# The low parts of the weights of four groups, made by GpSimd in place of VectorE

## What is computed

```python
h = rms_norm(x, g_mix)
z = h @ w_in + b_in                      # 1024 x 7168
va, ga, xb, gb, sa, sb = split(z)        # xb, gb: 1536 channels each
u = causal_conv31(va * sigmoid(ga))      # 1024 channels
v = rg_lru(causal_conv4(xb), ...)        # gates by block-diagonal products, then a scan over time
y_b = (v * gelu(gb)) @ w_b_out           # 1536 -> 1024
m = sigmoid(sa) * y_a + sigmoid(sb) * y_b
...                                      # output product, feed-forward, second block, final norm
```

## Time and profile before

| what | value |
|---|---|
| median of 3 runs | 2438.41 us (2437.18 to 2440.22) |
| profiled execution | 2438.8 us, its span 2436.6 us |
| TensorE matmul busy | 2410.2 us, 99% of the span |
| VectorE busy | 1405.1 us, 58% |
| ScalarE busy | 822.2 us, 34% |
| GpSimd busy | 2.2 us |
| TensorE clock granted | 0.998 of full over the span |

### The profile page before, as it was taken

How to read it: one execution, slowest core, us unless ns; L and a number is a source line. 1 busy time by engine, 2 the same in 40 slices (tenths; PEclk the granted TensorE clock), 3 DMA queues, 4 the chain that set the end, 5 groups by cost and what they waited for, 6 DMA issues and landing times.

```text
span 2436.6 us, 26080 instructions
## 1 busy us (share of the span) xinstructions
PE 2410.2 (99%) x10904; PEld 1958.8 (80%) x10904; DVE 1405.1 (58%) x1952; ACT 822.2 (34%) x1236; POOL 2.2 (0%) x7
## 2 busy tenths in 40 slices
PE   8999999999999999999999999999999999999998
PEld 6778688687778888888888888888878877888888
DVE  8799599698689734443233232234557544462377
ACT  5552442533513713332032131132333132122355
POOL 0000000000000000000000000000000000000000
PEclk9999999999999999999999999999999999999999
DMA  4202112012131112311111111112211111211232
GB/s 136 57 22 59 55 35 75 26 44 74 35 104 44 44 52 74 91 52 51 45 52 44 52 44 52 50 46 70 78 37 55 44 36 44 56 52 49 73 81 80
DMA packets 225117, 138.38 MB, mean 57 GB/s; under 512 B 13024, under 2 KB 216160, under 8 KB 225000
## 3 DMA queue, kind: packets, MB, share of 16 engines
q1 hardware_dynamic: 225000, 136.72, 19.0%
HBM read 127.75 MB, written 8.95 MB: 56 GB/s over the span
## 4 chain that ended last, share of the span: by engine, by line
PE 88%; DVE 6%; ACT 4%; issue 1%; DMA 0%; SPq 0%; DVEq 0%; ACTq 0%
PE bank L601 27%; PE bank L603 27%; PE bank L602 27%; PE bank L671 2%; DVE q_all L2528 1%; PE bank L912 1%; DVE uw L2318 0%; PE bank L894 0%; ACT whi L1045 0%; ACT bank L1148 0%; DVE wlo L1672 0%; DVE uc L2045 0%; ACT lru L1151 0%; PE bank L941 0%; ACT un_hi L1054 0%
## 5 line engine op out<-in xcount | busy, mean ns | idle before, releaser
L601 PE MATMUL bank<-h_hi,whi 128*128 128x512 f32 x1984 | 782.2, 394 | 10.0 <-DVE wlo L1672 10.0
L603 PE MATMUL bank<-h_hi,wlo 128*128 128x512 f32 x1984 | 774.6, 390 | 0.0
L602 PE MATMUL bank<-h_lo,whi 128*128 128x512 f32 x1984 | 774.4, 390 | 0.0
L601 PEld LDWEIGHTS bank<-h_hi,whi 128*128 128x128 f32 x1984 | 373.7, 188 | 91.5 <-issue 11.9
L602 PEld LDWEIGHTS bank<-h_lo,whi 128*128 128x128 f32 x1984 | 373.7, 188 | 79.4 <-issue 2.9
L603 PEld LDWEIGHTS bank<-h_hi,wlo 128*128 128x128 f32 x1984 | 373.5, 188 | 77.8
L1045 ACT ACTIVATE whi<-raw 128x1024 fp32r<-128x1024 f32 (+1 forms) x211 | 215.2, 1023 | 453.8 <-PE bank L603 419.4
L1672 DVE TENSOR_TENSOR wlo<-raw,whi 128x1024 fp32r<-128x1024 f32 (+1 forms) x211 | 249.5, 1185 | 170.9 <-ACT whi L1045 169.7
L601 PE MATMUL bank<-ff_hi,whi 128*128 128x512 f32 x512 | 199.9, 390 | 0.0
L602 PE MATMUL bank<-ff_lo,whi 128*128 128x512 f32 x512 | 199.5, 390 | 0.0
L603 PE MATMUL bank<-ff_hi,wlo 128*128 128x512 f32 x512 | 199.5, 390 | 0.0
(11 more groups left out here) (365 smaller groups left out, 3105.0 us busy)
## 6 DMA issues: line engine op xcount, KB each, us to landing
raw<-in_w_in SPq DMA_DIRECT2D x92, 512.0 KB, 3.7
raw<-in_w SPq DMA_DIRECT2D x64, 512.0 KB, 4.0
raw<-in_w_b_out SPq DMA_DIRECT2D x16, 384.0 KB, 3.0
raw<-in_w_out SPq DMA_DIRECT2D x11, 512.0 KB, 3.5
x_in<-in_x_t SPq DMA_DIRECT2D x8, 512.0 KB, 7.0
raw<-in_w_a_out SPq DMA_DIRECT2D x8, 512.0 KB, 3.9
raw<-in_w_o SPq DMA_DIRECT2D x8, 512.0 KB, 4.2
xcols<-in_x_t SPq DMA_DIRECT2D x16, 256.0 KB, 2.8
```

Of the source, the lines that this page charges most:

```text
L601: pe.matmul(target, lh, rh, start=start, stop=False, skip_group_check=True)
L602: pe.matmul(target, lh, rl, start=False, stop=False, skip_group_check=True)
L603: last = pe.matmul(target, ll, rh, start=False, stop=stop and point is not None, skip_group_check=True)
```

## The change

The low parts of blocks `("gb", 0, 2)` to `("yb", 3, 3)`, numbers 5 to 57 of the list (37 blocks of 1024 columns and 16 of 768), are made by GpSimd. VectorE's `ahead` passes over them, and makes those of all other blocks as before. GpSimd works through the 53 blocks in their order, each as soon as its high part is made and its buffer is free, between its first clears and its last one.

```diff
+        BY_POOL = range(number["gb", 0, 2], number["yb", NG - 1, 3] + 1)
...
                 while split[0] <= min(k, last_block):
                     i = split[0]
                     split[0] += 1
+                    if i in BY_POOL:
+                        continue
                     raw_, hi, lo = weight_tiles(i)
                     w.wait_ge(*at("w_hi", i))
...
             w = Once(pool)
             for n in range(2):
                 pool.memset(gate_w[n][:], 0.0).then_inc(*up("pool_done", ("gate_w_clear", n)))
+            for i in BY_POOL:
+                raw_, hi, lo = weight_tiles(i)
+                w.wait_ge(*at("w_hi", i))
+                w.wait_ge(*at("used", i - 3))
+                pool.tensor_tensor(lo, raw_, hi.bitcast(F32), ALU.subtract).then_inc(*up("pool_done", ("w", i)))
             w.wait_ge(*at("w1", FC - 1, DT - 1, 1))
             pool.memset(gates_raw[:], 0.0).then_inc(*up("pool_done", ("cleared",)))
```

## The result

The changed kernel took 2465.86 us (median of 4 runs, 2463.29 to 2467.39), the kernel before 2437.8 us in the same comparison: ratio 1.011, interval 1.0098 to 1.0122, so slower by 28 us. The profiled execution took 2466.36 us, 27.6 us more than that of before.

The account below looks back on a forecast made before the run. TensorE, busy 99% of the span, was taken as the bound. To the profiled 2438.8 us came three groups' losses of 4.6 us less 1.9 us (+11.9) and 2.5 us of clock: 2453 us, range 2436 to 2478.

Parts of the forecast that it names:

- the likeliest case: VectorE stands still during each GpSimd subtraction, delaying TensorE at the `yb` banks: 2453 us, chance 0.58.
- The bound and the tight place: TensorE bounds; VectorE delays over about 2 us between 136 and 208 us reach it at `yb` in groups 0 to 2.
- The mutual hold: VectorE and GpSimd share SBUF access; VectorE was taken to stand for each whole GpSimd subtraction, the upper bound.
- Rival 1: No mutual hold: GpSimd works beside VectorE, only the wait for L1913 goes; 2437 us, chance 0.25.
- The time of a subtraction: On GpSimd, 2.06 us for 1024 columns and 1.56 for 768, between VectorE's time and three streams in turn.
- The sum ahead of bank 0: From 136 to 208 us, seven holds of 12.4 us against 6.0 freed: VectorE 6.4 us late, TensorE loses 4.6.
- 6.0 freed: Time off VectorE's queue from 136 to 208 us: six low parts removed, three of 1.13 and three of 0.87 us.
- 1.86 of slack: Group 0, `yb` bank 0: VectorE's read ends at 208.83 us, TensorE takes the bank again at 210.69.
- The clock: TensorE's pauses may halve its clock: 5 us for three groups, of which half, 2.5 us, was taken.
- Group 3: VectorE's waits ahead of the `yb` blocks go, pieces start earlier, and TensorE's 1.9 us wait for L1913 goes.
- The range: 2436 to 2478 us: the hold between its bounds (2437 to 2476) plus no mutual hold, without GpSimd starving.
- Rival 2: GpSimd gets its turn only when VectorE stops; low parts late, some 21 us a group, 2500 us, chance 0.11.

Follow-up runs that it names:

- run 3: Changed kernel, but VectorE again makes the 24 low parts ahead of the tight `yb` banks in groups 0 to 2, GpSimd the other 29: 2435.31 us, ratio 0.9988.
- run 4: Changed kernel, but GpSimd makes only the 24 low parts ahead of the tight `yb` banks in groups 0 to 2, VectorE all others: 2468.56 us, ratio 1.0126.
- run 1: Changed kernel, but GpSimd clears each of the 53 low parts instead of subtracting, so it reads nothing: 2435.29 us, ratio 0.9989.
- run 2: Changed kernel, but GpSimd copies raw into each low part, reading one input instead of two: 2434.65 us, ratio 0.9988.
- run 5: Changed kernel, with 18 convolution pieces in each of groups 0 to 2 moved from ahead of the `yb` blocks to the next group: 2434.83 us, ratio 0.9987.
- run 6: Changed kernel, but GpSimd makes only three low parts in each of groups 0 to 2: 2442.18 us, ratio 1.0018.
- run 8: Kernel before, nothing on GpSimd; in group 3 VectorE's `ahead` at the two sb blocks goes behind the convolution pieces: 2435.49 us, ratio 0.9988.

## Why the prediction was right, and where it was short

2453 us was forecast, with 2436 to 2478 as the range; 2465.86 came. The direction and the likeliest case were right, the size was half: + 14.4 us on the profiled execution, against 27.6.

- *The bound and the tight place.* Right. TensorE waits at `yb` bank 8, for bank 0's read, in groups 0, 1 and 2 alone. Runs 3 and 4 show that the place decides: 29 subtractions elsewhere cost nothing, 24 here cost all.
- *The mutual hold.* Right, and shown: it is there with two inputs (2.14 us) and with one (0.79), and absent when GpSimd only writes (runs 1 and 2), always for VectorE's operations with two inputs. Rival 1 is out for reading operations. The Trainium skill (SBUF — State Buffer, section SBUF: two separate sides) excludes VectorE's two-input instructions only against GpSimd operations that read SBUF; these traces agree, with 0.759 us for the longest `evens` piece of the run with clears and 2.89 us for a piece beside a subtraction.
- *The time of a subtraction.* Nearly right, in part by luck: 2.06 and 1.56 us were taken, the middle of two bounds, for the operation and the hold alike. The operation by itself takes more, 2.34 us (656.66) and 1.84 (705.57), and VectorE stands for less than that: 2.14 (2.08 on the scan) and, at 768 columns, 1.58 at a piece (2.33 in place of 0.75).
- *The sum ahead of bank 0.* This step failed in its count. "From 136 to 208 us seven high parts are made" held for the old timing of bank 0. The holds push that read to 217.50 us, and by then an eighth subtraction, of 1024 columns, has started at 212.16. The prediction added it only on the way to bank 8. Holds measured in group 0 ahead of bank 0: 2.14 + 2.08 + 2.14 + 1.58 + 1.66 + 1.34 + 1.58 + 2.08 = 14.6 us, less 6.0 freed = 8.6; the other 0.75 us of the 9.35 late are small gaps, such as VectorE's wait for its own last piece ahead of L1795, which a low part used to fill. Less 1.86 of slack: 7.5 us (the profile has a wait of 7.30), against 4.6 forecast. Three groups: 22.1 us of waits in place of 13.8. Run 5, where the read comes early and seven subtractions precede it, bears the count out.
- *The clock.* This term was too small. Half of 5 us was taken, and more than the 5 came: 2.4 to 2.5 us a group, 7.5 in all, of which about 0.1 us a group is the first matmul's longer step, which is there at full clock too (run 6). Run 6 has pauses of 1.3 us at a clock of 1.00, so the cost came with the long pauses and not with the short ones; where between them it begins, no run shows. It is not the length of a pause alone: around 1768 us the clock fell with no pause over 0.5 us, behind sixteen matmuls of one column.
- *Group 3.* Right in size and cause: 1.9 us back, and run 8 shows that it is the queue's order.
- *Together:* 22.1 of waits and 7.5 behind them; that is all but 0.1 to 0.2 us a group of the 10.0 us by which each of groups 0 to 2 is longer. The first matmul behind the `yb` blocks comes 10.05, 20.06 and 30.07 us later than before (in groups 1 and 2 at 415.12 and 592.67 us, against 395.06 and 562.60). Group 3 gives 2.1 us back, the 1.9 of the wait for L1913 among them. 30.0 - 2.1 = 27.9 us is the difference of the two spans (2464.5 and 2436.6), and nothing is left for the start or for the stages behind.
- *The range.* It held, but not for its own reason: its upper end came from a subtraction of 2.89 us, and the excess came from an eighth hold and from the clock.
- *Rival 2, GpSimd starves.* Not in groups 0 to 2, but it is real: see below.

## What to carry to other kernels

An operation moved from VectorE to GpSimd need not be off VectorE if both read SBUF: here one of 1.13 us in the queue came back as a hold of 2.14 us. Whether that costs anything is a matter of place: find the bank or buffer with the least slack, and count the holds up to the moment at which it is read after the delay, not before it. And look first whether the queue's own order has the same gain to give: two lines swapped gave back the wait of 1.9 us that the change was able to remove.

## What had not been expected of the hardware

**The turn goes either way.** In groups 0 to 2 GpSimd was let in after the VectorE instruction under way. Ahead of group 3's `yb` blocks it was not. The timeline of GpSimd, and VectorE's groups from 690 to 702 us:

```profile
683.81 4.61 POOL L2621 TENSOR_TENSOR wlo<-raw,whi 128x768 fp32r<-128x768 f32 x1 [7.95 <-ACT whi L1047]
694.69 7.26 POOL L2621 TENSOR_TENSOR wlo<-raw,whi 128x768 fp32r<-128x768 f32 x1 [6.27 <-ACT whi L1047]
705.57 1.84 POOL L2621 TENSOR_TENSOR wlo<-raw,whi 128x768 fp32r<-128x768 f32 x1 [3.62 <-ACT whi L1047]
```

```profile
L1869 DVE SCALAR_TENSOR_TENSOR odds<-u_in,par,odds 128x512 f32<-128x512 f32 x6 | 4.5, 744 | 0.0
L1862 DVE SCALAR_TENSOR_TENSOR evens<-u_in,par,evens 128x513 f32<-128x513 f32 x5 | 3.7, 747 | 0.0
```

The same operation takes 1.84, 4.61 and 7.26 us, while VectorE's pieces keep their 0.745 us. The one of 7.26 us ended at 701.95; VectorE ran out of pieces at 700.25, 1.70 us before that. The one of 4.61 us ended at 688.42, 1.74 us after VectorE had gone from pieces to L1908, which reads a bank (686.68); the piece behind that, at 687.88, took 1.10 us. So for most of its time GpSimd stood, and VectorE did not. In run 5 one of 1024 columns took 6.59 us within such a row of pieces. What decides who waits was not tried and stays open; both outcomes occur amid the same kind of instructions. No wait of TensorE came of it, the low parts being made well ahead. Had the holds of groups 0 to 2 gone this way, with the low parts still in time, VectorE would not have been late at all and the forecast would have had the wrong sign; that is argued, not run.

**An instruction with one input from SBUF is held too.** L1795 took 2.15 us in place of 0.81. The instructions that read a bank, L1917 at 713.07 us, ran beside GpSimd at their usual length:

```profile
713.07 1.28 DVE L1917 SCALAR_TENSOR_TENSOR yb<-bank,yb 128x512 f32<-128x512 f32 x2
```

```profile
713.44 1.85 POOL L2621 TENSOR_TENSOR wlo<-raw,whi 128x768 fp32r<-128x768 f32 x1 [6.03 <-ACT whi L1047]
```
